# Dense weight stream of a backbone kernel: three raw buffers and three high halves in place of four and two

## The reference

```
for i in range(DEPTH):                       # DEPTH = 2
    mod_x = silu(c) @ w_mod[i] + b_mod[i]    # six shifts, scales and gates of 1024
    hx = modulate(rmsnorm(x, norm1_w[i]), mod_x[:, 0], mod_x[:, 1])
    if i % 2 == 0: yx, yc = ssd_mixer(hx, hc, ...)      # w_in, conv of 5 taps, 8 groups, scan, w_out
    else:          yx, yc = window_attention(hx, hc, ...)
    x = x + mod_x[:, 2][:, None] * yx
    hx = modulate(rmsnorm(x, norm2_w[i]), mod_x[:, 3], mod_x[:, 4])
    if i % 2 == 0: f = swiglu(h, w1, w3, w2)            # D_FF = 2816
    else:          f = moe_swiglu(h, router, w1, w3, w2) # 8 experts, D_FF_EXPERT = 3584
    x = x + mod_x[:, 5][:, None] * f
return rmsnorm(x, final_norm_w)
```

## Time and profile before

| | us |
|---|---|
| median of 3 runs (2247.83 to 2248.93) | 2248.43 |
| the profiled execution: its time | 2248.92 |
| its span | 2246.8 |
| PE busy in the span | 2117.8 (94%) |
| DVE busy | 1465.2 (65%) |
| ACT busy | 1231.6 (55%) |
| POOL busy | 52.2 (2%) |

### The profile page before, as it was taken

The page is one execution under the profiler, slowest core; times in us unless marked ns, Lnnn a source line. Parts: engine busy times, 40 slices in busy tenths (PEclk is TensorE's granted clock), DMA queues, the critical chain, the costliest instruction groups (busy, mean ns, idle before and its releaser), DMA issues.

```text
span 2246.8 us, 26971 instructions
## 1 busy us (share of the span) xinstructions
PE 2117.8 (94%) x11268; PEld 1709.3 (76%) x11268; DVE 1465.2 (65%) x1389; ACT 1231.6 (55%) x1376; POOL 52.2 (2%) x20
## 2 busy tenths in 40 slices
PE   6889999979899999998887999999999999999997
PEld 4677878757677777887676788888888888888885
DVE  3567777763323332325546888888888988888885
ACT  4567666652322222215545766776766766776763
POOL 0011111100000000000000000000000000000000
PEclk9999999979899999998997999999999999999998
DMA  7233344432144444322305899899898999899891
GB/s 308 97 116 147 141 147 182 183 118 75 59 185 150 177 161 166 121 98 98 130 1 229 349 340 358 336 367 350 341 355 343 352 340 358 337 367 349 342 354 56
DMA packets 71777, 510.08 MB, mean 227 GB/s; under 512 B 7968, under 2 KB 8352, under 8 KB 10976
## 3 DMA queue, kind: packets, MB, share of 16 engines
q1 hardware_dynamic: 71568, 508.15, 59.7%
q10 hardware_dynamic: 80, 0.13, 0.0%
HBM read 504.97 MB, written 3.28 MB: 226 GB/s over the span
## 4 chain that ended last, share of the span: by engine, by line
PE 82%; DVE 8%; ACT 4%; issue 1%; DVEq 0%; ACTq 0%
PE ps L1087 14%; PE ps L1085 14%; PE ps L1086 14%; PE ps L659 10%; PE ps L661 10%; PE ps L660 10%; DVE area L1799 3%; DVE d_lo L1670 2%; ACT area L1324 1%; PE ps L1069 1%; PE ps L1116 1%; PE ps L671 1%; PE ps L756 1%; PE ps L1146 1%; ACT d_hi L1256 1%
## 5 line engine op out<-in xcount | busy, mean ns | idle before, releaser
L2118 DVE TENSOR_TENSOR w_lo<-w_raw,w_hi 128x2048 fp32r<-128x2048 f32 x336 | 748.5, 2287 | 59.1 <-ACT w_hi L1546 59.1
L1546 ACT ACTIVATE w_hi<-w_raw 128x2048 fp32r<-128x2048 f32 x336 | 625.3, 1919 | 77.0 <-PE ps L1087 75.7
L1670 DVE TENSOR_TENSOR d_lo<-d_raw,d_hi 128x2048 fp32r<-128x2048 f32 (+1 forms) x76 | 171.9, 2262 | 329.8 <-ACT d_hi L1256 329.8
L1085 PE MATMUL ps<-w_hi,x_hi 128*128 128x512 f32 x896 | 358.1, 400 | 5.1 <-DVE x_lo L2173 5.1
L1087 PE MATMUL ps<-w_hi,x_lo 128*128 128x512 f32 x896 | 356.0, 397 | 0.0
L659 PE MATMUL ps<-h_top,d_hi 128*128 128x512 f32 (+1 forms) x816 | 331.3, 406 | 25.2 <-DVE h_low L1662 9.8
L1086 PE MATMUL ps<-w_lo,x_hi 128*128 128x512 f32 x896 | 351.6, 392 | 0.0
L1256 ACT ACTIVATE d_hi<-d_raw 128x2048 fp32r<-128x2048 f32 (+1 forms) x76 | 143.8, 1891 | 373.1 <-DMA d_raw<-in_dense 235.7
L661 PE MATMUL ps<-h_top,d_lo 128*128 128x512 f32 (+1 forms) x816 | 322.8, 396 | 0.0
L660 PE MATMUL ps<-h_low,d_hi 128*128 128x512 f32 (+1 forms) x816 | 318.9, 391 | 0.0
L659 PEld LDWEIGHTS ps<-h_top,d_hi 128*128 128x128 f32 x816 | 158.3, 194 | 69.6 <-issue 26.2
(11 more groups left out here) (289 smaller groups left out, 2487.9 us busy)
## 6 DMA issues: line engine op xcount, KB each, us to landing
w_raw<-in_experts SPq DMA_DIRECT2D x336, 1024.0 KB, 4.8
d_raw<-in_dense SPq DMA_DIRECT2D x120, 1024.0 KB, 5.3
area<-acum_rows SPq DMA_DIRECT2D x16, 1024.0 KB, 7.6
d_raw<-in_dense SPq DMA_DIRECT2D x4, 768.0 KB, 4.3
xT<-in_xt SPq DMA_DIRECT2D x4, 512.0 KB, 6.4
gate_rows<-area SPq DMA_DIRECT2D x4, 512.0 KB, 6.8
hT<-gate_rows SPq DMA_DIRECT2D x2, 1024.0 KB, 6.2
cst<-in_consts SPq DMA_DIRECT2D x2, 512.0 KB, 12.1
```

Of the source, the lines that this page charges most:

```text
L1085: mm(o, hi, w_hi[u % HIGH][:, a:a + 512], start=first, stop=False)
L1546: A(w_hi[n % HIGH][:], w_raw[n % RAW][:], ACT.Copy).then_inc(S["whi_done"], 1)
L1670: TT(d_lo[u][:, 0:w], d_raw[u][:, 0:w], d_hi[si % D_HIGH][:, 0:w].bitcast(F32), ALU.subtract)\
L2118: TT(w_lo[n % RAW][:], w_raw[n % RAW][:], w_hi[n % HIGH][:].bitcast(F32), ALU.subtract)\
```

## The change

One of the six places of the ring region goes from the raw buffers to the high halves. With it, four units in place of five are loaded before the list's first wait.

```diff
-D_RAW = 4
-D_HIGH = 2
+D_RAW = 3
+D_HIGH = 3
...
-        d_raw_at = [place_of["ring"] + 4 * o for o in (0, 2048, 8192, 10240)] + [place_of["area"]]
-        d_hi_at = [place_of["ring"] + 4 * o for o in (4096, 6144)]
+        d_raw_at = [place_of["ring"] + 4 * o for o in (0, 2048, 8192)] + [place_of["area"]]
+        d_hi_at = [place_of["ring"] + 4 * o for o in (4096, 6144, 10240)]
...
-            d_in0 d_in1 d_in2 d_in3 d_in4 d_used dhi_done dlo_done ghi_done glo_done hidhi_done hidlo_done
+            d_in0 d_in1 d_in2 d_in3 d_used dhi_done dlo_done ghi_done glo_done hidhi_done hidlo_done
...
-            for n in range(4):
+            for n in range(D_RAW):
                 load_dense(n)
             load_dense(D_AT[EARLY])
...
-                if n < 4 or unit == EARLY:
+                if n < D_RAW or unit == EARLY:
```

## The result

| | us | range, runs |
|---|---|---|
| before | 2248.01 | 2247.83 to 2248.93, 5 |
| changed | 2335.45 | 2331.35 to 2340.79, 5 |
| ratio | 1.0388 | 95% interval 1.0374 to 1.0402 |

What follows compares the result with a forecast made beforehand. PE, busy 94% of the span, bounds the kernel, so only its waits matter. 2.5 + 56 + 4.1 + 6.5 + 2.7 + 2 - 6.5 = +67 us gives 2316 against 2248.4; own range 2297 to 2333, 8 in 10 within 2290 to 2340.

Steps and rivals of the forecast that it cites:

- the two signs of being wrong: Group loop's cycle stays below 55 us, or the feed-forward's places stall by more than 0.5 us each.
- The cycle: Group loop, z used to z used: 59.7 us for 50.4; six cost +56, bounds +41 and +70.
- pass 0's chain: First pass of the group loop, row transfers' issue to bc's start: 21.2 us, basis for the 23.2 taken in later passes.
- The clock: Second rival, group loop: 1.2 GHz lasts longer, in bc and z; +76 in six cycles, 2336 us; chance 0.13.
- Feed-forward: The two loads after each unit swap roles, DVE's comes second; +2 us for 21 places, bounds 0 and 11.
- the cover of 2.9 us: Feed-forward: DVE's copy was ready at 726.93, PE needs it at 729.85; the later load uses this up.
- The start: Startup up to z1 used: nothing from startup itself, z1 late once by 2.5 us.
- the forecast stall: Ahead of z: its load goes out when bc is used, so PE stalls 2.6 us.
- wout, norm, attention: After the loop: wout(1,0)'s later load +6.5 us, w3(0)'s delaying the norm +2.7, wait ahead of attention -4.1.
- Group 7's part: Last group: its exponentials end at z used + 22.3 in place of +18.2, costing +4.1 us.
- late rows: Group loop: row transfers queue behind a load waiting for z, going out at z used + 0.4 us instead of - 11.3.
- my first rival, rows absorbed: Group loop: row transfers' lateness is absorbed, 4.5 us per pass, 27 in six; 2283 us; chance 0.12.

Runs made afterwards that it cites:

- without the hold: Kernel before with z's load held until bc is used, row transfers at their early place, no added wait on POOL: 2305.89 us.
- With the hold: Kernel before with z's load held until bc is used, plus a POOL wait putting masks after DVE's modulation result: 2283.3 us.
- rows late alone: Kernel before, four raw buffers, with only the row transfers moved behind loads or waits that wait for z used: 2288.3 us, ratio 1.0181.
- the rows early: Changed kernel with each group's row transfers issued ahead of the load that waits for z used: 2325.46 us, ratio 1.0346.

## Why the prediction was right, and where it was off

**The verdict and the mechanism** were right: slower, within the range, by the steps forecast. The sum was 67 and the profile has 82.6. The size was less right than the verdict: 2335.45 is above the 2297 to 2333 that the forecast gave itself by its bounds, the range of 2290 to 2340 holds it by 4.5 us, and one run of five, 2340.79, lies outside. One of the two signs of being wrong also came: 12 places of the feed-forward part stall, by 0.83 us on average, where the limit was 0.5. Against the forecast, the profile has +2.0 in the cycles, +12.8 in the feed-forward part, +3.1 at the start and -1.8 from z7 to the norm.

**The cycle** was 59.7 by four terms; it is 60.0. Each term, mean of the six passes, read from the timeline at L748, L659, L634 and L643:

| term | predicted | measured | before |
|---|---|---|---|
| z used to bc's start | 23.2 | 23.2 (22.7 to 24.1) | 18.6 |
| bc with the states | 15.9 | 14.7 (13.9, or 15.4 to 15.5) | 13.9 |
| bc used to z's start | 9.2 | 10.0 (9.3 to 10.4) | 6.65 |
| z | 11.4 | 12.2 (11.25 or 12.6 to 12.8) | 11.24 |

The first, taken from pass 0's chain, is the one on which most rested, and it held. The clock's share was put on bc alone; it fell on bc in half of the passes and on z in four of six. The load of z took the forecast 4.9 us from issue to landing in the first two of these passes, and PE's stall was 2.6. In the last four it took 5.8 to 6.0 and the stall was 3.5 to 3.7: there SP issues a spill (L538) 0.4 us behind it, which I left out (for z(4), the load at 314.96 and the spill at 315.34; before, too, z(4)'s load, at 268.67 with the spill at 269.05, took 5.8). The errors of the four terms cancel, and that the sum comes out within 0.3 us is luck.

**The clock** as a rival gave 2336, which is by its number the best of all, and by its reason it is not. It wanted +76 in the cycles, which have 58.0. PE's busy time in them rose by 14.8 us (292.08 to 306.88), so the slower clock is at most a quarter of the loop's loss. By the table 0.8 of it in bc and 1.0 in z lie on the cycle, some 11 us in six; the rest falls ahead of bc, where PE has time to wait. My forecast held some 12, as 2.0 a pass in bc (15.9 for 13.9). The missing 16 us are elsewhere.

**Feed-forward**, predicted +2 with bounds 0 and 11, is +14.8, and this is the term that was mis-sized. Its mechanism (the unit that DVE needs first lands second) was right, and so was the cover of 2.9 us that it uses up. Two things in it were wrong.

First, the landing. "Ready at about 729.8" against a need at 729.85 was taken for a stall of nothing. That is 4.7 us (high half, low half, copy) counted from 725.1, but in the trace of before the second load of that pair, issued at 718.73, landed 7.2 us later, at 725.89. With the same 4.7 us behind it the copy is ready at 730.6, 0.7 us late. Measured is a stall in 12 places, 0.83 us on average, 9.9 us in all. It is 12 of some 21 because a stall relieves the next place. The timeline of ACT and PE, 803 to 815 us, after:

```profile
803.78 1.91 ACT L1256 ACTIVATE d_hi<-d_raw 128x2048 fp32r<-128x2048 f32 x1 [12.30 <-DMA d_raw<-in_dense]
808.47 0.61 PE L682 MATMUL ps<-cst 128*128 128x2 f32 x4 [0.83 <-DVE cst L1684]
814.95 1.92 ACT L1256 ACTIVATE d_hi<-d_raw 128x2048 fp32r<-128x2048 f32 x1 [8.29 <-DMA d_raw<-in_dense]
```

The load used at 803.78 was issued 1.37 us behind its pair's first and took 7.4 us. The stall at 808.47 holds back the use of the mod unit, and with it the next such load: it goes out 2.47 us behind its pair's first, takes 4.8 us, and PE does not wait at the next L682. Then a pair is 1.37 us apart again, and the next place stalls. This alternation goes on through most of the stretch.

Second, the clock. The other 4.9 us are PE's busy time (291.75 to 296.65); before, the clock had stayed at 1.00 throughout this stretch. One window of the changed kernel (columns as above), behind a stall of 1.57 us at 954.76, has a busy PE at half its clock:

```profile
957.00:958.00 1.00, 1.00 (x4) 0.81 (x3) 0.00 (x0) 0.00 (x0) 0.00 (x0) 0.50 1.29 295
```

What failed is the price of a used-up cover: the landing was read 0.8 us too early, and what a stall can cost in clock was not in it at all.

**The start**, predicted at nothing beside z1's 2.5, is +5.6. The outputs of group 0 begin 1.7 us late (136.86 for 135.2). In this stretch PE waits 2.48 us at 27.96 for the fourth m0 unit, which before was loaded ahead of the constants; I had argued that DVE hides it, and L643 behind it starts 1.4 later (30.71 for 29.31). From the outputs on z1 loses another 4.0: 2.6 are the forecast stall, the rest again a longer z (12.6 for 11.24).

**wout, norm, attention** came as forecast: 6.4 for 6.5 at L643, 2.4 for 2.7, -4.1 for -4.1. Group 7 and the projection together took 7.2 for 9.0. Group 7's part is the smaller one: the product at L659 that waits 9.58 us (7.75 before) starts 3.4 later against z7 used, for 4.1, and 0.6 of that is won back in the product itself. Behind L643 2.0 are won, for 1.6.

**What the prediction did not see** is the overlap of POOL and DVE. It cost nothing in the changed kernel, since late rows had moved the masks out of the convolution, so that the forecast did without it by luck. It would have been missed in any forecast of one half of the change: my first rival, rows absorbed, had 27 us for the loop, and without the hold the loop of that kernel took 55.6 more than before. With the hold it took 29.2.

Left open: in which gaps the clock falls. With rows late alone, gaps ahead of bc of 5.03 and 5.15 us were followed by 15.47 and 16.51 us of bc, one of 3.50 by 13.93; in the changed kernel one of 3.18 was followed by 15.50 and one of 3.29 by 13.91. So the length of the gap alone does not decide it.

## What to carry to other kernels

A buffer taken from a ring costs where a transfer of another kind stands behind the ring's wait in the same queue; list for every wait what is queued behind it, and try the queue's order before the ring's size. When the removal of a wait gives nothing, look whether the duration of instructions on the other engines changed: the wait may have kept two engines apart. And a cover that comes out at zero is a stall: take the landing from the trace and not from a window, ask whether one stall relieves the next place, and price with it the clock that the engine may lose.

## What the hardware showed that was not expected

POOL's masks (affine select, 128x2048, from and to on-chip memory) and DVE's convolution (a scalar_tensor_tensor with two such inputs) do not share, they exclude each other. A mask by itself takes 2.00 us; where DVE was in its eight operations of 745 ns it took up to 5.45 us, and DVE lost nothing. Where the mask was first, DVE lost 3.5 us in a convolution, in its first two operations of 2.48 to 2.51 us each. One wait on POOL, which by itself does nothing useful, made kernels 22.6 and 27.7 us faster. The Trainium skill (SBUF — State Buffer, "SBUF: two separate sides") describes this as an exclusive lock, which a DVE operation with two inputs there and a GpSimd one that reads there hold for a whole instruction, "the other fully blocks"; the traces agree in both directions. They add that POOL, once DVE was in its eight operations, got in only after the last: in one pass of the kernel before, its first mask took 5.38 us from 250.48, and the convolution, five of whose operations began after 250.48, ended at 253.99. With the rows early it got in ahead of the first operation and again ahead of the second. What decides where it gets in is not shown.

Also, the changed kernel's runs spread over 9.4 us and those of the kernel before over 1.1 us. Within its one profile a pass takes 57.1 to 62.3 us, where before all took 50.0 to 50.6.
